# Attention's orders on ScalarE and SyncE, and pooling's first inputs loaded during attention

## The chip, the cores and the metric

The kernel runs on 1 core of a Trainium2 chip. The metric is the device time of one execution, in microseconds (us), with all inputs in HBM and the output written back to HBM. Runs differ by a few tenths of a per cent, so a median of several stands for a kernel.

## What is computed

One layer of a hybrid encoder on 2048 tokens of width 1024, in float32: three token mixers side by side (pooling, differential attention, a state-space layer), gates from the same normalised input, an output projection, and then a mixture of experts.

```python
h = modulate(rmsnorm(x, norm1_g[l]), sh1, sc1)
u_a, q, k, v, u_c = jnp.split(h @ w_in[l], splits, axis=-1)
ya = pool_mixer(u_a, pool_w[l], pool_scale[l])
yb = diff_attention(q, k, v, cos, sin, ...)          # 4 heads, 2 maps each, block-causal
yc = ssm_mixer(u_c, ...)
ga, gb, gc = jnp.split(jax.nn.sigmoid(h @ gate_w[l] + gate_b[l]), 3, axis=-1)
mixed = ga * (ya @ proj_a[l]) + gb * (yb @ proj_b[l]) + gc * (yc @ proj_c[l])
x = x + g1[:, None, :] * (mixed @ w_out[l])
x = x + g2[:, None, :] * hier_moe(h2, ...)           # top-1 group, top-2 experts
```

Attention, for a query block of 128 tokens: both maps are a softmax over the keys that the mask allows, a = p0 - lam * p1, and the result is a @ v. Pooling, for a group of 64 channels with window w of 2, 4, 8 or 16: the mean of the last w tokens minus the token, times a 64x64 matrix, times a scale per channel:

```python
cnt = jnp.minimum(t, float(w))[None, :, None]
outs.append((cg - prev) / cnt - ug[:, :, g])
y = jnp.einsum('bsgc,gcd->bsgd', pooled, pool_w).reshape(B, S, POOL_WIDTH)
return y * pool_scale
```

## The kernel before

The program is a chain of stages: projection, attention, pooling, state space, merge and output, experts. Each stage has one instruction stream per engine, written out by hand, with semaphores between the engines, and it ends with a barrier of all engines. An engine works strictly in the order of its stream, so an instruction that waits holds up all that stand behind it.

**Attention** runs over 4 heads (h = 0 to 3) and in each over 16 blocks of 128 queries (i = 0 to 15, called blocks 0 to 15 here). A block's keys come in chunks of 512. For a block TensorE makes the scores of both maps (L303), VectorE evacuates them and takes the maxima (L518, L521, `maxima` L529 and L530), ScalarE takes the exponentials of map 1 and map 0 (`exps`, L427), VectorE weighs the maps against each other (`weigh`, L542), TensorE turns the result by 128x128 blocks (`turn_a`, L313), ScalarE copies a chunk of turned blocks (`place`, L435), and TensorE multiplies them by v (`weigh_v`, L324). `take` (L440, L443) reads the block's result, and at a head's end all 16 are normed (L486), turned, split into a high and a low part and stored by SyncE as y. The scores of block i + 2 and the exponentials of block i + 1 stand inside block i.

**Gates fill TensorE's gaps.** The gate matmul goes by columns of 128 outputs (24 columns, c) and halves of 512 tokens: a gate unit (48 in attention, `gu`) is 8 groups of 3 matmuls (L336 to L338, high by high, high by low, low by high) that sum in one PSUM bank, bank 7. `gate_plan` gives in `slots[i]` how many groups stand in block i: the first number ahead of the block's turns, and then one for each chunk of keys, behind the turn of that chunk. A unit can't begin before ScalarE has read bank 7 (`gate_out`, L418). After each second unit `gate_out` also rounds the next column's weights to their high part (`w_high`, L412); VectorE then makes the low part (`lower`, L555), and SyncE may load the raw column after that (`load_w`, L248, 512 KB into one buffer). SyncE stores each gate output (`store_gates`, L256).

In block 3 the last group of unit 3 stands behind the only turn, and in block 14 the last group of unit 8 stood in the second chunk's slot (behind the second chunk's `turn_a` and ahead of the first chunk's `weigh_v`). In block 15 the last group of unit 9 stands in the third chunk's slot.

**SyncE** issues all the loads and stores, in one queue. Per head it goes over 12 gate units (u = 0 to 11). At u = 8 it waits for all scores of the head and loads q and k of the next one (16 loads, 4 MB; in the last head the late half of h, 4 MB). At u = 11 it stores y. At the stage's end it clears 128 rows of `acc` in HBM (512 KB) and waits for everything that is under way.

**Pooling** has two blocks of 128 channels (c = 0, 1), each of 2048 tokens. VectorE makes the window sums by doubling (`wider`, L814, L815) and the difference (L830 to L835). TensorE multiplies each 512 tokens by a 128x128 matrix with two 64x64 blocks in it (L788), ScalarE scales (L804) and rounds (L806), VectorE makes the low part (L840), SyncE stores both. Six gate units fill TensorE here too (`GateFill`): units 0 and 1 ahead of block 0's products, units 2, 3 and 4 ahead of block 1's, unit 5 at the end. Unit 2 is the first to use the late half of h. `GateFill.out` reads a unit out and, after each second one, calls `higher` for the next raw column (`gw_hi`); GpSimd makes the low part (`lower`, L691), and only then does SyncE load another (`load_next`, L652). SyncE's stream began with: u block 0 (1 MB), late half of h (2 MB high, 2 MB low), the scales (256 values), four 64x64 matrices, u block 1 (1 MB), a raw gate column, two blocks of uc (1 MB each).

## Time and profile before

| what | us |
|---|---|
| median of 3 runs (lowest, highest) | 2951.82 (2948.14, 2960.63) |
| the profiled execution, its own time | 2954.11 |
| its span (first to last instruction) | 2952.2 |
| TensorE busy in the span | 2782.0 (94%) |
| VectorE, ScalarE, GpSimd busy | 1905.2, 1469.0, 369.0 |
| granted TensorE clock, mean | 0.968 of full speed |

By stage, TensorE was busy for 607.37 of 631 us in attention (469 to 1100), not at all between 1100 and 1106 (the change of stages), for 45.65 of 57 us in pooling (1107 to 1164), and for 1695.84 of the 1788 us behind. Over attention the clock was at 0.99 of full speed, over pooling at 0.88.

A row of the views in order of time has the start in us from the span's start, the length in us, the engine, the line, the operation, output <- input, and the count; in brackets stands how long the engine had been idle before it, and whose instruction ended that. PE is TensorE's matmuls, PEld its weight loads, DVE VectorE, ACT ScalarE, POOL GpSimd, SPq SyncE's queue of transfers. Matmuls are pipelined, so a matmul of 512 columns shows 0.39 us but starts 0.23 us after the one before.

### The profile page before, as it was taken

To read this page: it belongs to the slowest core of one execution; us is meant where nothing else is said; L and a number is where in the kernel's file an instruction comes from. 1 tells how busy PE (TensorE), PEld (TensorE's weight loads), DVE (VectorE), ACT (ScalarE), POOL (GpSimd) and SP (SyncE) were. 2 spreads that over 40 slices of the span, in tenths; PEclk is the share of its full clock that TensorE was granted. 3 is DMA by queue.
4 is the path that set the end of the run, shared out by engine and by line. 5 is a ranking of instruction groups with operands and counts; after the bars stand their busy time and mean duration, and the time that the engine had idled before them with its cause. 6 is when DMAs were issued, how large, how long until landed. Compare 5 with 4: busy or idle time off the path is not lost. (4 is left out here: it accounts for less than half of the span.)

```text
span 2952.2 us, 41275 instructions
## 1 busy us (share of the span) xinstructions
PE 2782.0 (94%) x13642; PEld 2215.4 (75%) x13643; DVE 1905.2 (65%) x3149; ACT 1469.0 (50%) x2361; POOL 369.0 (13%) x287
## 2 busy tenths in 40 slices
PE   6999998999999988999998999987999999999996
PEld 5768886787877776788876878875777777777774
DVE  6754774746464655644455773457888888888884
ACT  4414664656565553233244342124666666666662
POOL 2101220000000001101010001110222222222211
PEclk8999999999999998999999999998999999999998
DMA  6475324040403137211148995428989989777884
GB/s 234 143 248 193 105 103 164 23 155 31 154 30 129 44 125 237 68 47 50 51 168 295 352 343 204 168 93 301 337 280 298 374 299 304 239 226 228 283 258 134
DMA packets 287584, 554.82 MB, mean 188 GB/s; under 512 B 28748, under 2 KB 95564, under 8 KB 285144
## 3 DMA queue, kind: packets, MB, share of 16 engines
q1 hardware_dynamic: 269048, 492.06, 46.7%
q0 software_dynamic: 14400, 52.44, 7.2%
q10 hardware_dynamic: 4000, 8.53, 0.9%
q8 instruction: 82, 1.34, 0.2%
q14 instruction: 54, 0.44, 0.1%
HBM read 418.21 MB, written 143.15 MB: 190 GB/s over the span
## 5 line engine op out<-in xcount | busy, mean ns | idle before, releaser
L2715 DVE TENSOR_TENSOR moe_w_lo<-moe_W,moe_w_hi 128x1024 fp32r<-128x1024 f32 x384 | 460.4, 1219 | 85.6 <-ACT moe_w_hi L2643 71.7
L2643 ACT CAST moe_w_hi<-moe_W 128x1024 fp32r (+1 forms) x384 | 402.0, 1052 | 148.1 <-PE moe_h1b L2566 76.2
L1631 PE MATMUL project_bank<-h_lo,w_hi 128*128 128x512 f32 x512 | 201.0, 393 | 0.0
L336 PE MATMUL att_bank<-h_hi,w_hi 128*128 128x512 f32 x384 | 168.9, 440 | 13.0 <-ACT att_gates L418 8.1
L2591 PE MATMUL moe_yb<-moe_W,moe_hT 128*128 x384 | 172.5, 592 | 0.0
L427 ACT ACTIVATE att_S<-att_S,att_nm,q_scale 128x128 f32<-128x128 f32 (+15 forms) x128 | 165.7, 1296 | 4.4 <-DVE att_nm L530 4.0
L2564 PE MATMUL moe_h1b<-moe_w_hi,moe_xT_hi 128*128 128x512 f32 x384 | 155.9, 406 | 4.8 <-DVE moe_xT_lo L2726 4.8
L521 DVE TENSOR_SCALAR_CACHE_REDUCE att_S<-att_bank 128x512 f32<-128x512 f32 x192 | 122.3, 687 | 54.8 <-PE att_bank L303 54.8
L338 PE MATMUL att_bank<-h_hi,w_lo 128*128 128x512 f32 x384 | 151.4, 394 | 0.0
L337 PE MATMUL att_bank<-h_lo,w_hi 128*128 128x512 f32 x384 | 151.2, 394 | 0.0
L2566 PE MATMUL moe_h1b<-moe_w_hi,moe_xT_lo 128*128 128x512 f32 x384 | 151.1, 393 | 0.0
L2565 PE MATMUL moe_h1b<-moe_w_lo,moe_xT_hi 128*128 128x512 f32 x384 | 151.0, 393 | 0.0
L2566 PE MATMUL moe_h3b<-moe_w_hi,moe_xT_lo 128*128 128x512 f32 x384 | 149.6, 389 | 0.0
L2564 PE MATMUL moe_h3b<-moe_w_hi,moe_xT_hi 128*128 128x512 f32 x384 | 149.4, 389 | 0.0
L2565 PE MATMUL moe_h3b<-moe_w_lo,moe_xT_hi 128*128 128x512 f32 x384 | 149.4, 389 | 0.0
L324 PEld LDWEIGHTS att_bank<-att_val,att_aT 128*128 128x128 f32 x1088 | 137.7, 191 | 14.1 <-ACT att_aT L435 5.1
L324 PE MATMUL att_bank<-att_val,att_aT 128*128 128x128 f32 x1088 | 145.0, 278 | 1.2 <-ACT att_aT L435 1.2
L698 ACT ACTIVATE gate_out<-ssm_gate_bank,gate_bias 128x512 f32<-128x512 f32 x42 | 28.9, 687 | 211.8 <-PE ssm_gate_bank L714 209.6
L2720 DVE TENSOR_TENSOR moe_w_lo<-moe_W,moe_w_hi 128x1024 fp32r<-128x1024 f32 x96 | 117.2, 1222 | 25.6 <-ACT moe_w_hi L2650 24.7
L435 ACT COPY att_aT<-att_bank 128x512 f32<-128x512 f32 (+3 forms) x160 | 82.8, 517 | 99.8 <-PE att_bank L313 99.3
L2591 PEld LDWEIGHTS moe_yb<-moe_W,moe_hT 128*128 128x128 f32 x384 | 72.6, 189 | 72.8 <-issue 69.0
L303 PE MATMUL att_bank<-shared 64*128 64x512 f32 (+2 forms) x960 | 124.3, 388 | 2.3 <-DVE att_S L521 2.3
(498 smaller groups left out, 6866.8 us busy)
## 6 DMA issues: line engine op xcount, KB each, us to landing
moe_W<-in_moe_w SPq DMA_DIRECT2D x96, 2048.0 KB, 13.8
w_raw<-in_gate_w SPq DMA_DIRECT2D x48, 512.0 KB, 3.8
out_sg<-gateT SPq DMA_DIRECT2D x32, 768.0 KB, 6.9
gateT<-att_gates SPq DMA_DIRECT2D x48, 256.0 KB, 2.0
gateT<-gate_out SPq DMA_DIRECT2D x48, 256.0 KB, 2.0
early<-in_ada_w SPq DMA_DIRECT2D x8, 1024.0 KB, 12.7
project_spare<-in_x SPq DMA_DIRECT2D x16, 512.0 KB, 6.9
zT<-project_oz SPq DMA_DIRECT2D x32, 256.0 KB, 3.5
```

Source lines behind the costliest of these rows:

```text
L324: mm = pe.matmul(bank[6][:, 0:P], aT[:, n % 2, j, :], val[:, 4 * c + j, :], start=4 * c + j == 0, stop=4 * c + j == i)
L336: pe.matmul(bank[7][:], w_hi[b][:, k, :], h_hi[:, k, at], start=k == 0, stop=False)
L337: pe.matmul(bank[7][:], w_hi[b][:, k, :], h_lo[:, k, at], start=False, stop=False)
L338: mm = pe.matmul(bank[7][:], w_lo[b][:, k, :], h_hi[:, k, at], start=False, stop=k == KD - 1)
L427: nc.scalar.activation(S[:, at, m, :n], S[:, at, m, :n], ACT.Exp, bias=nm[:, at, m:m + 1], scale=g["q_scale"][:, item // NT, item % NT, m: ...
L1631: pe.matmul(bank[n % 4][:], w_hi[b][:, k, :], low[:, k, at512(tb)], start=False, stop=False)
L2564: pe.matmul(to[:], xT_hi[:, k, :], w_hi[:, at, part], start=k == 0, stop=False)
L2565: pe.matmul(to[:], xT_hi[:, k, :], w_lo[:, at, part], start=False, stop=False)
L2566: mm = pe.matmul(to[:], xT_lo[:, k, :], w_hi[:, at, part], start=False, stop=k == KD - 1)
L2591: mm = pe.matmul(yb[nh][:], hT[:, k - KS, :], raw_2(at_raw, k, nh * 512, 512), start=False, stop=k == KF - 1)
L2643: nc.scalar.copy(w_hi[:, slot(p, first), :], raw(at, p)).then_inc(q["w13_high"], 1)
L2715: nc.vector.tensor_tensor(w_lo[:, own, :], raw(at, p), w_hi[:, own, :].bitcast(F32), ALU.subtract).then_inc(q["w1_low" if p < 4 else "w3_l ...
```

## The change

- ScalarE: in blocks 0 to 3 of each head both exponentials of the next block stand right behind `place`, ahead of the gate output. `w_high` is taken out of `gate_out` into `next_high`, with the same place everywhere but block 15, where it stands behind the next `place`.
- TensorE: one gate group of block 14 moves from the second chunk's slot to the first's, so ScalarE's gate output moves too. (In `slots[14]` the second and third numbers change places.)
- SyncE in attention: the load of the next raw column stands at the start of a unit (`next_w`), so at u = 8 it comes ahead of the q and k loads. At u = 5 of head 1 SyncE loads pooling's matrices and scales. At u = 1 of head 3, where there is no v left to load, it loads pooling's u block 0, into the place of vT, and clears the rows of `acc`.
- Pooling: u block 0, matrices and scales are there; SyncE's stream begins with u block 1, the late half of h, the raw column, uc. On ScalarE `higher` for the second raw column stands behind block 0's copies instead of ahead of them.
- Places in SBUF: vT, the matrices and the scales lie in tiles that both stages hold, and `first` and two empty rooms are sized so that the rest lies where it did.

```diff
@@ gate_plan
-             [1, 0, 1, 1, 0], [1, 0, 1, 1, 0], [1, 0, 1, 2, 1], [2, 1, 1, 1, 0]]
+             [1, 0, 1, 1, 0], [1, 0, 1, 1, 0], [1, 1, 0, 2, 1], [2, 1, 1, 1, 0]]
@@ attention, tiles
-        vT = s.sb("vT", [P, T])
+        s.sb("vT_room", [P, T])
+        vT = pool_in["u0"]
@@ attention, SyncE
+                def next_w(gu):
+                    if gu % 2 == 0:
+                        sp.wait_ge(q["w_split"], gu // 2 + 1)
+                        load_w(gu // 2 + 2)
+
                 def store_gates(gu):
                     c = gu // 2
-                    if gu % 2 == 0:
-                        sp.wait_ge(q["w_split"], c + 1)
-                        load_w(c + 2)
                     sp.wait_ge(q["gate_placed"], gu + 1)
...
                 for h in range(HEADS):
                     for u in range(NU):
+                        next_w(NU * h + u)
                         if u == units_by(NT - 3):
...
                         store_gates(NU * h + u)
-                        if u == 1 and h + 1 < HEADS:
+                        if h == 1 and u == 5:
+                            sp.wait_ge(q["pool_zeroed"], 1)
+                            for gr in range(4):
+                                at = slice((gr % 2) * 64, (gr % 2) * 64 + 64)
+                                sp.dma_start(pool_in["w"][at, gr // 2, at], g["pool_w"][0, gr]).then_inc(q["pool_ready"], 16)
+                            cols(nc, sp, pool_in["scale"][:], g["pool_scale"], 2, q["pool_ready"])
+                        if u == 1:
                             sp.wait_ge(q["v_turned"], TB * (h + 1))
-                            load_v(h + 1)
+                            if h + 1 < HEADS:
+                                load_v(h + 1)
+                            else:
+                                sp.dma_start(vT[:], g["zT"][0]).then_inc(q["u0_ready"], 16)
+                                sp.dma_start(g["acc"][T:T + P, :]..., zero[:]...).then_inc(q["cleared"], 16)
                 sp.wait_ge(q["raw_ready"], 16 * HEADS * CH)
-                sp.dma_start(g["acc"][T:T + P, :]..., zero[:]...).then_inc(q["cleared"], 16)
                 sp.wait_ge(q["cleared"], 16)
+                sp.wait_ge(q["u0_ready"], 16)
+                sp.wait_ge(q["pool_ready"], 16 * 5)
@@ attention, ScalarE
                         for n in range(lo, hi):
                             place(h, n)
+                            if high_after:
+                                next_high(high_after)
+                                high_after = 0
+                            if i < 4:
+                                exps(item + 1, 1)
+                                exps(item + 1, 0)
                             done += slots[i][1 + n - lo]
                             while placed < done // KD:
                                 gate_out(placed)
+                                if i == NT - 1:
+                                    high_after = placed
+                                else:
+                                    next_high(placed)
                                 placed += 1
-                            if n == lo and i + 1 < NT:
+                            if n == lo and 4 <= i < NT - 1:
                                 exps(item + 1, 1)
-                            if n == min(lo + 1, hi - 1) and i + 1 < NT:
+                            if n == min(lo + 1, hi - 1) and 4 <= i < NT - 1:
                                 exps(item + 1, 0)
@@ pooling, SyncE
-                sp.dma_start(ua[:, 0, :], g["zT"][0]).then_inc(u_ready[0], 16)
+                sp.dma_start(ua[1][:], g["zT"][1]).then_inc(u1_ready, 16)
                 sp.dma_start(h_hi[1][:].bitcast(F32), ...).then_inc(h_ready, 16)
                 sp.dma_start(h_lo[1][:].bitcast(F32), ...).then_inc(h_ready, 16)
-                cols(nc, sp, ps_col[:], g["pool_scale"], 2, small)
-                sp.wait_ge(zeroed, 1)
-                for gr in range(4):
-                    at = slice((gr % 2) * 64, (gr % 2) * 64 + 64)
-                    sp.dma_start(pw[at, gr // 2, at], g["pool_w"][0, gr]).then_inc(small, 16)
-                sp.dma_start(ua[:, 1, :], g["zT"][1]).then_inc(u_ready[1], 16)
                 fill.load_next(sp, 0)
@@ pooling, TensorE and ScalarE
-                    if n == 0:
-                        pe.wait_ge(small, 16 * 5)
...
                     if tb == 0:
+                        if c == 1:
+                            fill.higher(act, 1)
                         for u in ((0, 1), (2, 3, 4))[c]:
-                            fill.out(act, u)
-                    if n == 0:
-                        act.wait_ge(small, 16 * 5)
+                            fill.out(act, u, split=u != 1)
```

What stands in a row, at three places. First ScalarE in block 3 of head 1 (`att_S` of 128x640 are block 4's exponentials, `att_aT` is the copy of the turned blocks). Before:

```order
L443 ACTIVATE att_osq,att_ss<-att_bank,att_rec 128x128
L435 COPY att_aT<-att_bank 128x512
L418 ACTIVATE att_gates<-att_bank,gate_bias 128x512
L412 CAST w_hi<-w_raw 128x1024
L427 ACTIVATE att_S,att_den<-att_S,att_nm,q_scale 128x640 x2
L440 ACTIVATE att_o<-att_bank,att_rec 128x128
L443 ACTIVATE att_osq,att_ss<-att_bank,att_rec 128x128
```

and with the change:

```order
L464 ACTIVATE att_osq,att_ss<-att_bank,att_rec 128x128
L456 COPY att_aT<-att_bank 128x512
L448 ACTIVATE att_S,att_den<-att_S,att_nm,q_scale 128x640 x2
L437 ACTIVATE att_gates<-att_bank,gate_bias 128x512
L431 CAST w_hi<-w_raw 128x1024
L461 ACTIVATE att_o<-att_bank,att_rec 128x128
L464 ACTIVATE att_osq,att_ss<-att_bank,att_rec 128x128
```

The two exponentials of 128x640 moved ahead of the gate output and the cast.

Second TensorE in block 14 of head 0 (`h_hi`, `h_lo`, `w_hi`, `w_lo` are a gate group, `consts,att_S` a turn with one matmul for each 128x128, `att_val,att_aT` the product with v). Before:

```order
L337 MATMUL att_bank<-h_lo,w_hi 128x512
L338 MATMUL att_bank<-h_hi,w_lo 128x512
L313 MATMUL att_bank<-consts,att_S 128x128 x8
L336 MATMUL att_bank<-h_hi,w_hi 128x512
L337 MATMUL att_bank<-h_lo,w_hi 128x512
L338 MATMUL att_bank<-h_hi,w_lo 128x512
L324 MATMUL att_bank<-att_val,att_aT 128x128 x4
L313 MATMUL att_bank<-consts,att_S 128x128 x4
L336 MATMUL att_bank<-h_hi,w_hi 128x512
L337 MATMUL att_bank<-h_lo,w_hi 128x512
```

and with the change:

```order
L356 MATMUL att_bank<-h_lo,w_hi 128x512
L357 MATMUL att_bank<-h_hi,w_lo 128x512
L332 MATMUL att_bank<-consts,att_S 128x128 x4
L355 MATMUL att_bank<-h_hi,w_hi 128x512
L356 MATMUL att_bank<-h_lo,w_hi 128x512
L357 MATMUL att_bank<-h_hi,w_lo 128x512
L332 MATMUL att_bank<-consts,att_S 128x128 x4
L343 MATMUL att_bank<-att_val,att_aT 128x128 x4
L332 MATMUL att_bank<-consts,att_S 128x128 x4
L355 MATMUL att_bank<-h_hi,w_hi 128x512
```

The gate group moved from behind the two turns to between them.

Third ScalarE at pooling's start. Before:

```order
L698 ACTIVATE gate_out<-pooling_gate_bank,gate_bias 128x512 x2
L684 CAST gw_hi<-w_raw 128x1024
L804 ACTIVATE pooling_ya<-pooling_bank,pooling_ps_col 128x512
L806 CAST pooling_ya_hi<-pooling_ya 128x512
L804 ACTIVATE pooling_ya<-pooling_bank,pooling_ps_col 128x512
L806 CAST pooling_ya_hi<-pooling_ya 128x512
L804 ACTIVATE pooling_ya<-pooling_bank,pooling_ps_col 128x512
```

and with the change:

```order
L733 ACTIVATE gate_out<-pooling_gate_bank,gate_bias 128x512 x2
L829 ACTIVATE pooling_ya<-pooling_bank,pool_scale_in 128x512
L831 CAST pooling_ya_hi<-pooling_ya 128x512
L829 ACTIVATE pooling_ya<-pooling_bank,pool_scale_in 128x512
L831 CAST pooling_ya_hi<-pooling_ya 128x512
L829 ACTIVATE pooling_ya<-pooling_bank,pool_scale_in 128x512
L831 CAST pooling_ya_hi<-pooling_ya 128x512
L829 ACTIVATE pooling_ya<-pooling_bank,pool_scale_in 128x512
L831 CAST pooling_ya_hi<-pooling_ya 128x512
L719 CAST gw_hi<-w_raw 128x1024
L733 ACTIVATE gate_out<-pooling_gate_bank,gate_bias 128x512 x2
```

The cast `gw_hi` moved from ahead of block 0's four pairs of scale and cast to behind them.

## Rows read from the trace of the kernel before

**Rows 1.** Who waited, TensorE, attention and pooling: us in total, times, longest.
```profile
PE att_bank L313 <- DVE att_S L542: 9.6, 4, 2.4
PE att_bank L336 <- ACT att_gates L418: 8.1, 7, 1.4
...
PE pooling_bank L788 <- DMA pooling_pw<-in_pool_w: 6.0, 1, 6.0
```

**Rows 2.** In order of time, ScalarE, head 1, block 3: start, us, instruction.
```profile
658.11 0.59 ACT L435 COPY att_aT<-att_bank 128x512 f32<-128x512 f32 x1 [1.12 <-PE att_bank L313]
662.35 0.69 ACT L418 ACTIVATE att_gates<-att_bank,gate_bias 128x512 f32<-128x512 f32 x1 [3.65 <-PE att_bank L338]
662.94 1.04 ACT L412 CAST w_hi<-w_raw 128x1024 fp32r<-128x1024 f32 x1
...
664.79 0.91 ACT L427 ACTIVATE att_S<-att_S,att_nm,q_scale 128x640 f32<-128x640 f32 x1
```

**Rows 3.** In order of time, TensorE, head 1, turn of block 4.
```profile
667.22 0.66 PE L313 MATMUL att_bank<-consts,att_S 128*128 128x128 f32 x4 [2.41 <-DVE att_S L542]
```

**Rows 4.** In order of time, VectorE, head 1, around the weighing of block 4.
```profile
661.01 0.08 DVE L518 DVE_READ_ACCUMULATOR2_ANT att_mx<- 128x1 f32 x1
...
666.28 0.89 DVE L542 SCALAR_TENSOR_TENSOR att_S<-att_S,att_rec 128x640 f32<-128x640 f32 x1
```

**Rows 5.** In order of time, TensorE and its weight loads, head 1, blocks 14, 15.
```profile
757.87 0.50 PE L336 MATMUL att_bank<-h_hi,w_hi 128*128 128x512 f32 x1 [1.40 <-ACT att_gates L418]
...
761.29 1.72 PE L324 MATMUL att_bank<-att_val,att_aT 128*128 128x128 f32 x14
...
770.90 0.97 PEld L324 LDWEIGHTS att_bank<-att_val,att_aT 128*128 128x128 f32 x8 [0.17 <-ACT att_aT L435]
```

**Rows 6.** In order of time, ScalarE, head 1, block 14.
```profile
754.58 2.10 ACT L427 ACTIVATE att_S<-att_S,att_nm,q_scale 128x2048 f32<-128x2048 f32 x1
...
759.79 0.58 ACT L435 COPY att_aT<-att_bank 128x512 f32<-128x512 f32 x1
```

**Rows 7.** Who waited, SyncE's queue, attention and pooling.
```profile
SPq L256 <- ACT att_gates L418: 364.2, 44, 20.9
...
SPq L286 <- DMA gateT<-att_gates: 2.3, 1, 2.3
...
SPq L235 <- DMA acc<-att_zero: 1.5, 1, 1.5
```

**Rows 8.** In order of time, SyncE's queue, pooling's start.
```profile
1108.31 6.75 SPq L615 DMA_DIRECT2D pooling_ps_col<-in_pool_scale  x1
```

**Rows 9.** In order of time, TensorE, pooling.
```profile
1106.86 0.77 PE L712 MATMUL pooling_gate_bank<-shared,w_hi 128*128 128x512 f32 x1 [7.15 <-PEq L141]
...
1119.23 0.39 PE L714 MATMUL pooling_gate_bank<-shared,w_lo 128*128 128x512 f32 x1
...
1133.84 0.96 PE L712 MATMUL pooling_gate_bank<-late_hi,w_hi 128*128 128x512 f32 x1
...
1150.77 4.22 PE L788 MATMUL pooling_bank<-pooling_ua,pooling_pw 128*128 128x512 f32 x8
```

**Rows 10.** In order of time, ScalarE, pooling.
```profile
1129.30 1.04 ACT L684 CAST gw_hi<-w_raw 128x1024 fp32r<-128x1024 f32 x1 [8.96 <-DMA w_raw<-in_gate_w]
```

**Rows 11.** In order of time, VectorE, pooling.
```profile
1112.53 0.15 DVE L814 COPY pooling_A<-pooling_ua 128x1 f32<-128x1 f32 x1 [15.97 <-DMA pooling_ua<-zT]
...
1123.55 0.17 DVE L835 COPY pooling_first<-pooling_ua 128x16 f32<-128x16 f32 x1
1127.60 0.15 DVE L814 COPY pooling_A<-pooling_ua 128x1 f32<-128x1 f32 x1 [3.87 <-DMA pooling_ua<-zT]
...
1132.64 2.21 DVE L814 COPY pooling_A<-pooling_B 128x4 f32<-128x4 f32 x1
...
1145.71 0.17 DVE L835 COPY pooling_first<-pooling_ua 128x16 f32<-128x16 f32 x1
```

**Rows 12.** Transfers, pooling: issuer, count, KB each, us from issue to landing.
```profile
late_lo<-late_lo SPq DMA_DIRECT2D x1, 2048.0 KB, 17.0
```

More of the change, by code:

```diff
@@ L229, in stage_attention @@
                  "v_turned v_placed scored evacuated maxed exped scaled weighed a_turned a_placed "
-                 "summed o_copied o_squared o_rooted o_normed o_turned o_placed o_split y_stored lam_ready lam cleared late").split()
+                 "summed o_copied o_squared o_rooted o_normed o_turned o_placed o_split y_stored lam_ready lam cleared late pool_zeroed pool_ready u0_ready").split()
         q = {n: s.sem(n) for n in names}
@@ L287, in _ @@
                 sp.wait_ge(q["y_stored"], 32 * HEADS)
+            @block.gpsimd
+            def _(pool):
+                nc.gpsimd.memset(pool_in["w"][:], 0.0).then_inc(q["pool_zeroed"], 1)
             @block.tensor
@@ L692, in lower, with out @@
                                      self.tiles["w_hi"][b][:].rearrange("p k n -> p (k n)").bitcast(F32), ALU.subtract).then_inc(self.w_split, 1)
-    def out(self, act, u):
+    def out(self, act, u, split=True):
         act.wait_ge(self.summed, u + 1)
@@ L699, in out @@
                                   bias=self.tiles["gb"][:, self.c0 + self.unit(u)[0]:self.c0 + self.unit(u)[0] + 1]).then_inc(self.placed, 1)
-        if u % 2 == 1 and u // 2 + 1 < self.count:
+        if split and u % 2 == 1 and u // 2 + 1 < self.count:
             self.higher(act, u // 2 + 1)
@@ L787, in _ @@
                         pe.wait_ge(placed, n - 1)
-                    pe.matmul(bank[n % 2][:], pw[:, c, :], ua[:, c, tb * 512:(tb + 1) * 512], start=True, stop=True).then_inc(mixed, 1)
+                    pe.matmul(bank[n % 2][:], pw[:, c, :], ua[c][:, tb * 512:(tb + 1) * 512], start=True, stop=True).then_inc(mixed, 1)
                 for k in range(KD):
@@ L816, in _ @@
                 for c in range(2):
-                    dve.wait_ge(u_ready[c], 16)
-                    u = ua[:, c, :]
+                    if c == 1:
+                        dve.wait_ge(u1_ready, 16)
+                    u = ua[c][:]
                     wider(A[:], u, 1)
@@ L2982, in program @@
                 pass
+            with nc.sbuf_tensor("pool_u0", [P, T], F32) as u0:
+                pass
             with nc.sbuf_tensor("h_lo1", [P, KD, T // 2], F32R) as h_lo1:
```

43 lines of the change are left out of this document (25 added, 18 removed).

## The prediction

> **What bounds the kernel now.** I read three views in this order: who waited for whom on TensorE (attention and pooling alone), then the instructions in order of time on TensorE, ScalarE and VectorE around each long wait, then SyncE's queue and the transfers. TensorE holds this kernel: in attention its instructions stand back to back, and only a handful of waits cut them, so a microsecond taken from such a wait is a microsecond of the program, as long as the next engine in line isn't late too. [rows 1] gives the waits that the change aims at: 9.6 us in four waits for VectorE's weighing, 8.1 us in seven for ScalarE's gate outputs, and 6.0 us in one for pooling's matrices. The kernel is a chain of stages, with a barrier between attention, pooling and the state-space stage. What pooling's end gains moves the rest forward whole, since everything behind starts from that barrier.
>
> **Part 1, the exponentials ahead of the gate in block 3 of each head.** In [rows 2] ScalarE has copied block 3's turned weights at 658.11 and then stands until TensorE ends a gate unit; gate output (0.69), cast (1.04) and two exponentials (0.91 each) follow, so the sums that VectorE waits for come at about 665.8. In [rows 4] VectorE weighs at 666.28 for 0.89, and in [rows 3] TensorE goes on at 667.22, after 2.41 idle. The maxima for these exponentials were ready long before. Placed right behind the copy (0.59 long) they run from 658.7 to about 660.9. VectorE has the scores of the block after to evacuate until 661.1 [rows 4], then weighs until about 662.5. TensorE arrives at 667.22 - 2.41 = 664.8, so the wait goes whole. The gate output isn't delayed: the exponentials end 1.4 us ahead of its 662.35. What is late next? TensorE's scores and ScalarE's next copy follow TensorE's own time and shift with it. Four heads: 4 x 2.41 = **9.6 us**. Bounds: 9.6, and 4 x 1.5 = 6 if VectorE or ScalarE, shifted against each other, give back a microsecond in each head.
>
> **Part 2, block 14: one gate group from slot 2 to slot 1, its output ahead of the exponential.** TensorE loses 1.40 to the gate output in each head [rows 5]. ScalarE's row [rows 6] shows why: a 2.10 exponential stands at 754.58, then a copy, then the gate output. In the new order TensorE turns four blocks (through at about 754.0, when ScalarE's copy ahead of 754.58 began), runs the gate group (0.7, an eighth of a unit of 5.6), and ScalarE, free at 754.6, waits for it until about 755.1, puts the gate out (0.69) and starts the exponential at about 755.7. That is 1.1 later than 754.58. One gate output no longer stands between the two exponentials (0.6), so the rest of the queue is 0.55 later: the third copy begins not at 759.79 [rows 6] but at about 760.35, and ends at 760.95. TensorE needs it for the 14 products that start at 761.29 [rows 5]; 1.40 earlier would be 759.9. So it waits there instead, and starts at about 761.05. I keep 0.25 a head, **1.0 us** in all, with bounds of 0 and 4 x 1.4 = 5.6 us. Block 15's weights are ready at about 763.3, TensorE turns them at about 764.0: no wait there.
>
> **Part 3, block 15: the cast behind the copy.** TensorE's weight load waited 0.17 for that copy [rows 5]; 4 x 0.17 = **0.7 us**, between 0 and 0.7.
>
> **Part 4, SyncE's queue in attention.** The raw columns are loaded before the score wait and the 4 MB of q and k instead of behind them: nobody waits for them now, so nothing is gained or lost. The matrices and scales enter in head 1: the scales' issue alone holds the queue for 6.75 us [rows 8], the four matrix loads come on top. Behind them are the next raw column and the next gate stores. SyncE's cover is its waits for ScalarE's gate outputs, 364.2 us in 44, the longest 20.9 [rows 7]; without it the cost would be some 10 us once. The block of u (1 MB) and the cleared rows (512 KB) go out early in head 3, where the gate stores are the only traffic: nothing. The new tile places alone cost nothing: same sizes, same engines.
>
> **Part 5, the end of attention.** SyncE waited 2.3 us for the last gate store and then 1.5 us more for the cleared rows [rows 7]. The second goes: **1.5 us**, bounds 1.0 and 2.0.
>
> **Part 6, pooling.** I count from TensorE's first instruction, t = 0 at 1106.86 [rows 9]. Now: gate units 0 and 1 end at t = 12.7, TensorE waits 6.04 for the matrices [rows 1], then ScalarE stands 8.96 us until 1129.30 on a raw column queued behind everything else [rows 10], while four pooled products need its copies, and unit 2 starts at 1133.84, t = 27.0 [rows 9]. After the change:
> - VectorE starts at t = 0.2; now it waits to 1112.53 for u. Its chain for block 0 takes 1112.53 to 1123.72, 11.2 us [rows 11], so t = 11.4. GpSimd's lowering now runs beside it, at t = 1 to 5. In the other chain a 128x4 copy beside GpSimd took 2.21 us, where one of 128x16 takes 0.17 [rows 11]; I add 2.0, t = 13.4. The Trainium skill (GPSIMD Engine Reference, the quick-facts table) says that GpSimd's SBUF interfaces are shared with VectorE; by it the 2.0 stay, without it the products start at t = 12.7, and the sum is the same, because the next item ends last.
> - The second pooling block (eight matmul rows with their copies) takes 4.2 us [rows 9]. So the first is through at about t = 17.6.
> - Unit 2 needs the late half of h, two loads of 2 MB. The second took 17.0 us to land [rows 12]; it was issued just ahead of the scales' load at 1108.31 [rows 8], so it landed at t = 17.0 to 18.4, and I take 17.9. The 1 MB in front stays (it is now the other block of u). What changes is what is queued behind it: the raw column and uc now follow at t = 5 rather than 12. Bounds: 17 if the queue serves in order, and 22 if all 7.5 MB queued by then share the time. I take the first kind, since u, issued 0.5 us ahead of the 4 MB, was there at t = 5.7 [rows 11]. The Trainium skill (DMA: Bandwidth & Descriptors, Queues, rings and completion order) says each engine takes its descriptors in ring order; by it the 22 is excluded, and the sum is as forecast.
> - So unit 2 starts at t = 18.0 instead of 27.0: **9.0 us**, bounds 5.0 and 10.0.
> - Behind it: ScalarE's cast of the raw column follows the four copies at about t = 20, GpSimd has lowered it by about 25; unit 4 needs it at t = 29. VectorE's second chain takes 1127.60 to 1145.88, 18.3 us [rows 11], so it ends at t = 31.7, and TensorE wants it after three units (1133.84 to 1150.77, 16.9 us [rows 9]), at t = 34.9. The margin is 3.2 us, against 4.9 now.
>
> **The sum.** 9.6 + 1.0 + 0.7 + 1.5 + 9.0 = 21.8 us. The profiled execution took 2954.1 (span 2952.2), so 2932.3; against the median of 2951.8 it is 2930.0. I say **2931**. All of it lies in attention and pooling; the stages behind should show nothing.
>
> **The rivals.**
> A. The late half of h binds, and later than I say. For it: transfers are the densest thing in pooling, and more is queued at once. Against it: u's early landing. With h at t = 22, pooling gives 5.0 and the total 17.8; with 6 from part 1 as well, 14 us, 2940.
> B. The order of block 14 pays in full, since ScalarE gains time elsewhere (parts 2 and 5 at their upper ends, pooling at t = 17): 4.6 + 0.5 + 1.0 more, 28 us, 2926 from the profiled time and 2924 from the median.
> C. Slower: SyncE is stuck in head 1. The scales are 256 separate 4-byte elements. If SyncE's queue doesn't get past them before ScalarE needs raw column 11, ScalarE's cast waits, and TensorE behind it. The cover in one place is up to 20.9 us [rows 7]; each microsecond beyond it is one of the program. From 43 us on (20.9 + 21.8) the whole gain is gone, and an issue of 90 us would give 2954 + 47, about 3001. [rows 8] shows 6.75.
> D. The change doesn't do what it says: the exponentials in block 3 still come late, because what they wait for is not ScalarE's order but their maxima. Then 9.6 goes and 12.2 are left: 2940 to 2942. Against it: VectorE's evacuation at 661.01 is of the block after.
>
> **Chances.** Forecast (2924 to 2937) 0.72, A 0.12, B 0.06, D 0.07, C 0.03. A measurement of this kernel can tell about 0.5%, 14.8 us, from no change. A, D and the weak edge of the forecast lie near that bound: faster 0.83, within it 0.14, slower 0.03. The range runs from 2920 (B, from the fastest run shown, 2948) to 2944 (A and D, from a slower start): those leave out C and the combination of A with D.
>
> **What would show it.** On TensorE: no wait of 2.4 us ahead of the turn of block 4 in any head, and in block 14 a wait for the copy of about 1 us where the one for the gate output was. Last attention matmul some 11 us earlier. From it to pooling's first matmul about 5.6 us instead of 7.15. In pooling VectorE starts with the stage, no wait for matrices, and unit 2 at t = 18, released by the load of h. Part 6 is wrong if unit 2 starts after t = 20, or if TensorE waits for VectorE's second chain; part 2 if the new wait is missing (then up to 4.6 us more) or if a wait of over 1.4 us appears. The forecast as a whole is wrong if a stage behind pooling changes its length by more than 3 us.

## The result, and the profile after

The changed kernel takes 2925.9 us (median of 5 runs, 2924.8 to 2933.9) against 2951.8 (2948.1 to 2960.6). The ratio is 0.9912, with a 95% interval of 0.9898 to 0.9927: 26 us, 0.9% faster. The forecast was 2931 with a range of 2920 to 2944, so time and sign were right. Part of that is luck, since two misses of the sum cancel each other in part. By stages it was right less evenly, as this table of the two profiled executions shows. "Attention" runs from its first matmul to the end of its last, "pooling" from its first matmul to the state-space stage's first.

| stretch | before | after | change | forecast |
|---|---|---|---|---|
| to attention's first matmul | 468.8 | 464.3 | -4.5 | 0 |
| attention | 631.0 | 612.7 | -18.3 | -11.3 |
| attention's last to pooling's first matmul | 7.15 | 5.89 | -1.3 | -1.5 |
| pooling | 57.3 | 51.1 | -6.2 | -9.0 |
| everything behind | 1788.1 | 1789.1 | +1.0 | 0 |
| span | 2952.2 | 2923.0 | -29.2 | -21.8 |

TensorE's waits in attention and pooling, with the change (us in total, times, longest), are the answer to [rows 1]:

```profile
PE ssm_bank L999 <- PEq L141: 7.2, 1, 7.2
PE pooling_gate_bank L747 <- PEq L141: 5.9, 1, 5.9
...
PE att_bank L343 <- ACT att_aT L456: 3.3, 12, 0.4
PE att_bank L355 <- ACT att_gates L437: 2.6, 3, 0.9
PE att_bank L322 <- DVE att_S L556: 2.3, 4, 0.6
```

The line of 9.6 us for VectorE's weighing is gone, and so are pooling's matrices. Of the 8.1 us for gate outputs 2.6 are left (three heads' first unit). New are 3.3 us for ScalarE's copies (1.2 before), and the wait of 7.2 us ahead of the state-space stage, which had been 3.7.

ScalarE in order of time in block 3 of head 1, the answer to [rows 2]:

```profile
648.54 0.59 ACT L456 COPY att_aT<-att_bank 128x512 f32<-128x512 f32 x1 [1.12 <-PE att_bank L332]
649.02 0.92 ACT L448 ACTIVATE att_S<-att_S,att_nm,q_scale 128x640 f32<-128x640 f32 x1
...
649.94 0.91 ACT L448 ACTIVATE att_S<-att_S,att_nm,q_scale 128x640 f32<-128x640 f32 x1
...
652.78 0.69 ACT L437 ACTIVATE att_gates<-att_bank,gate_bias 128x512 f32<-128x512 f32 x1 [1.84 <-PE att_bank L357]
```

The two exponentials (L448) follow the copy at once and end at 650.85; the gate output comes 1.9 us later, when TensorE has ended its unit, and was not delayed. VectorE in the same place, the answer to [rows 4]:

```profile
651.88 0.88 DVE L577 SCALAR_TENSOR_TENSOR att_S<-att_S,att_rec 128x640 f32<-128x640 f32 x1
```

It is through at 652.8, before TensorE turns the block at 655.08, without a wait.

### The profile page after: what moved, and what is told of

The parts are those of the page before. It is cut to its first block and busy times, and to the rows that moved or that the text cites. A ratio compares the mean times of both kernels' runs of the same rounds, so it can differ in the third digit from the quotient of the medians.

```text
span 2923.0 us, 41275 instructions
## 1 busy us (share of the span) xinstructions
PE 2774.7 (95%) x13642; PEld 2209.9 (76%) x13643; DVE 1907.6 (65%) x3149; ACT 1468.3 (50%) x2361; POOL 372.4 (13%) x287
## 5 line engine op out<-in xcount | busy, mean ns | idle before, releaser
L448 ACT ACTIVATE att_S<-att_S,att_nm,q_scale 128x128 f32<-128x128 f32 (+15 forms) x128 | 165.8, 1296 | 4.5 <-DVE att_nm L565 4.0
L726 POOL TENSOR_TENSOR w_lo<-w_raw,w_hi 128x1024 fp32r<-128x1024 f32 x15 | 38.5, 2568 | 876.0 <-ACT w_hi L719 876.0
```

What stands on the lines that cost most here:

```text
L448: nc.scalar.activation(S[:, at, m, :n], S[:, at, m, :n], ACT.Exp, bias=nm[:, at, m:m + 1], scale=g["q_scale"][:, item // NT, item % NT, m: ...
```

## The experiments

Stage lengths in us, from the profile of each kernel, and the medians. All but the first two are the changed kernel with the edits told below. "Start of attention" is the time to its first matmul, "to pooling" that from its last matmul to pooling's first. The medians come from several chips, so kernels are compared by their ratios, each to the kernel before on its own chip, wherever the chips differ.

| kernel | start of attention | attention | to pooling | pooling | median (runs) | ratio to before, 95% |
|---|---|---|---|---|---|---|
| before, first profile | 468.8 | 631.0 | 7.15 | 57.3 | 2951.8 (5) | |
| before once more | 468.3 | 630.2 | 7.15 | 58.0 | 2953.0 (10) | 0.9988 to 1.0018 |
| changed | 464.3 | 612.7 | 5.89 | 51.1 | 2925.9 (5) | 0.9898 to 0.9927 |
| exponentials back | 464.6 | 628.5 | 5.86 | 51.1 | 2941.4 (8) | 0.9941 to 0.9971 |
| block 14 back | 465.6 | 615.0 | 5.86 | 51.0 | 2926.4 (4) | 0.9878 to 0.9924 |
| all attention orders back | 468.2 | 633.5 | 5.85 | 51.1 | 2946.1 (10) | 0.9957 to 0.9984 |
| exponentials back, waits filled | 467.6 | 622.9 | 5.85 | 51.0 | 2935.9 (4) | 0.9918 to 0.9959 |
| pooling's cast ahead | 468.0 | 613.3 | 5.88 | 53.5 | 2928.9 (4) | 0.9902 to 0.9938 |
| low parts early | 461.7 | 612.8 | 5.88 | 49.7 | 2919.3 (4) | 0.9874 to 0.9916 |
| low parts early, unit 5 split | 469.0 | 614.8 | 5.87 | 48.1 | 2923.7 (4) | 0.9877 to 0.9922 |
| raw column behind | 465.1 | 613.3 | 5.87 | 50.9 | 2927.2 (4) | 0.9897 to 0.9947 |
| clearing at the end | 468.3 | 612.2 | 7.51 | 51.0 | 2930.9 (4) | 0.9909 to 0.9960 |
| u block 0 in pooling | 468.7 | 615.7 | 5.89 | 53.6 | 2929.6 (4) | 0.9911 to 0.9952 |

**What moves without an edit.** The kernel before, run again:

> The kernel before once more, for what moves without an edit. The changed kernel's profile reached its first attention matmul 4.5 us earlier (464.28 against 468.75), in a stage with no edit. Theory: that is the spread between executions, so this profile's start lies anywhere in 463 to 470, while the attention stage itself (first to last matmul) is 631 us again, within 2. Rival: the new places of tiles in SBUF speed up the projection; then this profile starts attention at 468 to 469 again.

Attention began at 468.3, which by this one profile would have spoken for the rival. But over all the kernels here, of which none but the first two differs from the changed one ahead of attention, it begins anywhere between 461.7 and 469.0. Most of that spread is the granted clock: by the clock records of the traces TensorE lost between 9.6 and 15.4 us to half clock ahead of attention (15.4 in the kernel before, 10.4 in the changed one), and the start less this loss is 452 to 455 us in all thirteen profiles. So the 4.5 us ahead of attention are taken for the spread of single executions, and not for a gain of the change; the medians agree, since the three edited stretches alone give 18.3 + 1.3 + 6.2 = 25.8 us of the 25.9. With two profiles of the old tile places a mean difference of a microsecond or two isn't excluded. Everything behind pooling, edited nowhere either, took 1783.3 to 1793.8 us. So a stage in the middle is compared with itself, not by its place in the span.

**Exponentials back.**

```diff
                             place(h, n)
...
-                            if i < 4:
-                                exps(item + 1, 1)
-                                exps(item + 1, 0)
...
-                            if n == lo and 4 <= i < NT - 1:
+                            if n == lo and i + 1 < NT:
                                 exps(item + 1, 1)
-                            if n == min(lo + 1, hi - 1) and 4 <= i < NT - 1:
+                            if n == min(lo + 1, hi - 1) and i + 1 < NT:
                                 exps(item + 1, 0)
```

> The changed kernel with block 0 to 3's exponentials back behind the gate output. Theory: the four waits of 2.4 us return, and in the heads in which the granted clock falls to 1.2 GHz after the wait another 1.5 to 2 us, so attention is 9.6 + 3 to 6 = 13 to 16 us longer than with the change, 2939 to 2942. Rival (the prediction's sum): the waits alone, 9.6 us, clock at full behind them, 2935.5.

Attention takes 15.8 us more (628.5 against 612.7), the medians differ by 15.5. The waits are the old ones (total, times, longest):

```profile
PE att_bank L332 <- DVE att_S L574: 9.6, 4, 2.4
```

So 6.2 us come on top of the 9.6. The busy time by stretch tells from where: behind the stretch's length stand the busy us (and the number of instructions) of TensorE, its weight loads, VectorE, ScalarE and GpSimd, then the granted clock, the share of the DMA engines and GB/s. Behind the wait of head 2:

```profile
817.98:819.98 2.00, 2.00 (x14) 1.68 (x16) 1.56 (x4) 1.31 (x2) 0.00 (x0) 0.84 0.00 0
819.98:821.98 2.00, 2.00 (x8) 1.27 (x7) 2.00 (x8) 0.29 (x2) 0.00 (x0) 0.50 0.69 201
821.98:823.98 2.00, 2.00 (x10) 1.60 (x9) 0.01 (x1) 0.67 (x2) 0.00 (x0) 0.81 0.24 69
```

TensorE is busy all the time there, at 0.84, 0.50 and 0.81 of full speed. The same in the kernel before, head 2, whose first stretch is the wait itself:

```profile
820.77:823.17 2.40, 0.00 (x0) 0.00 (x0) 1.32 (x4) 1.58 (x6) 0.00 (x0) 1.00 0.00 0
823.17:825.17 2.00, 2.00 (x10) 1.50 (x12) 1.31 (x3) 1.17 (x2) 0.00 (x0) 0.60 0.00 0
825.17:827.17 2.00, 2.00 (x10) 1.38 (x9) 1.50 (x5) 0.43 (x2) 0.00 (x0) 0.55 0.71 207
827.17:829.17 2.00, 2.00 (x12) 1.60 (x11) 0.77 (x4) 0.70 (x2) 0.00 (x0) 1.00 0.23 64
```

In four microseconds at 0.60 and 0.55 of full speed 1.7 us of matmuls are lost. By the clock records it is one stretch of 3.4 us at half speed. The waits of 2.41 us are the same in all four heads of all four kernels that have them; the clock fell to the 1.2 GHz level behind three in the kernel before, two in its second profile, three here and all four with all orders back: 12 of 16. Three falls lose 3 x 1.7 = 5.1 us, which leaves 1.1 of the 6.2; a first wait for v at attention's start that was 0.6 longer in this profile is part of it.

**The waits filled.** Whether the idle time does it, or something else at that place, is told apart by taking the idle time away without the wait: TensorE turns a constant 16 times while it would wait.

```diff
+                        if i == 4:
+                            pe.wait_ge(q["a_placed"], NP * h + lo - 1)
+                            for _ in range(16):
+                                pe.transpose(bank[4 + lo % 2][:, :P], const(g, "ident"), const(g, "ident"))
                         pe.wait_ge(q["weighed"], NT * h + i + 1)
```

> The kernel of e1_no_exps (exponentials of blocks 0 to 3 back behind the gate output) with 16 turns of a constant, whose result nobody reads, on TensorE ahead of each of the four long waits, into the bank that the next turn overwrites. Theory (the wait of 2.4 us costs itself, and then the granted clock): the waits shrink to about 0.4 us by idle time but TensorE goes on at the same moment as in e1_no_exps, and the granted clock stays at 1.0 behind all four. Attention then takes 612.7 + 9.6 = 622.3 us instead of 628.5, the kernel 2935. Rival: the clock falls for another reason (the mix of work behind, or by the hour), then attention takes 628 to 630 again.

Attention takes 622.9 us, 0.6 from the forecast. TensorE, head 2, the 16 extra turns and what follows:

```profile
815.89 1.91 PE L399 MATMUL att_bank<-consts 128*128 128x128 f32 x16
818.46 0.66 PE L332 MATMUL att_bank<-consts,att_S 128*128 128x128 f32 x4 [0.66 <-DVE att_S L578]
```

and the stretches around it:

```profile
816.00:818.00 2.00, 1.80 (x17) 1.56 (x15) 0.86 (x3) 1.64 (x7) 0.00 (x0) 1.00 0.03 8
818.00:820.00 2.00, 1.54 (x12) 1.25 (x14) 1.77 (x4) 0.84 (x2) 0.00 (x0) 1.00 0.00 0
820.00:822.00 2.00, 2.00 (x16) 1.46 (x12) 1.86 (x7) 0.76 (x2) 0.00 (x0) 1.00 0.41 115
```

The real work goes on no sooner, since VectorE is as late as it was, but the clock stays at 1.00, here and behind the other three waits. The useless work made attention 5.6 us shorter than without it, and the three falls that are gone account for 5.1 of that. So of the 15.8 us some 10 are the waits and some 5 the clock. The stage lengths and the clock show this; the ratios of the two kernels (0.9939 and 0.9956) point the same way, but their intervals overlap.

**Block 14 back.**

```diff
-             [1, 0, 1, 1, 0], [1, 0, 1, 1, 0], [1, 1, 0, 2, 1], [2, 1, 1, 1, 0]]
+             [1, 0, 1, 1, 0], [1, 0, 1, 1, 0], [1, 0, 1, 2, 1], [2, 1, 1, 1, 0]]
```

> The changed kernel with block 14's gate group back in its slot. By the changed kernel's rows (0.17 + 0.37 of new waits where 1.40 was) 4 x 0.86 = 3.4 us come back: 2929.3. By the prediction's sum it would be 1.0 us: 2926.9.

Attention takes 2.3 us more, and the four waits of 1.4 for the gate output are back (8.1 in seven), the eight new ones for copies gone (1.2 in four). The medians differ by 0.5, which settles nothing, and attention itself varies by 3.5 us among kernels with the same order (612.2 to 615.7). That variation has a place: the two longest (614.8 and 615.7) waited 1.6 and 2.2 us for v at attention's start, with a fall of the clock behind it, the others 1.2 or less, without one. So the size is read from the stretch that the edit touches, from block 14's first gate group to the next head's first scores. In head 1, with block 14 back:

```profile
742.40 0.48 PE L355 MATMUL att_bank<-h_hi,w_hi 128*128 128x512 f32 x1
...
761.56 0.95 PE L322 MATMUL att_bank<-shared 64*128 64x128 f32 x12
```

and with the change:

```profile
740.47 0.48 PE L355 MATMUL att_bank<-h_hi,w_hi 128*128 128x512 f32 x1
...
759.04 0.95 PE L322 MATMUL att_bank<-shared 64*128 64x128 f32 x12
```

That is 19.16 and 18.57 us, and the other heads differ by 0.55 to 0.57 in the same stretch: 2.3 us in all. The idle time changed by 0.85 a head, close to the theory's 0.86, but this overstates the gain, since around the two new waits TensorE loses more than shows as idle (the 14 products behind the second take 1.83 us, where [rows 5] has 1.72). Neither the 3.4 nor the prediction's 1.0 came true. In the kernel before, and with all orders back, head 1's stretch takes 19.36 and 19.32, so the cast of block 15 is worth 0.2 a head.

ScalarE with the change, head 1, block 14:

```profile
742.59 0.69 ACT L437 ACTIVATE att_gates<-att_bank,gate_bias 128x512 f32<-128x512 f32 x1
...
747.81 0.96 ACT L456 COPY att_aT<-att_bank 128x512 f32<-128x512 f32 x2
```

and TensorE:

```profile
745.88 1.16 PE L343 MATMUL att_bank<-att_val,att_aT 128*128 128x128 f32 x8 [0.17 <-ACT att_aT L456]
...
748.44 1.83 PE L343 MATMUL att_bank<-att_val,att_aT 128*128 128x128 f32 x14 [0.37 <-ACT att_aT L456]
```

The gate output starts at 742.59, 0.1 us behind the copy and not 0.5: TensorE's group had begun at 741.61, before ScalarE started its copy (741.89). So the third copy (747.81) is 5.2 us behind the gate output's start, and TensorE waits for it 0.37, and 0.17 for the second.

**All attention orders back** (the exponentials' and block 14's edits above, and the cast of block 15 back in `gate_out`'s place):

```diff
-                                if i == NT - 1:
-                                    high_after = placed
-                                else:
-                                    next_high(placed)
+                                next_high(placed)
```

> The changed kernel with all of ScalarE's and TensorE's attention orders undone (exponentials, block 14, cast of block 15); SyncE's queue, the early loads and pooling stay changed. Theory: attention as long as before but for the last wait, 18 us more than the change, 2944; the parts add up (exponentials 13 to 16, block 14 3.4, cast 0.7). Rival: SyncE's new order carries a share, then this comes out at 2940 or less although the single undoings sum to 18.

Attention takes 20.8 us more than with the change. That is 2.5 more than in the kernel before, with the same waits and all four falls of the clock, the last of them longer than any other (0.50 for more than six microseconds). The single undoings add to 18.1, with the cast's 0.8 to 18.9. The four falls lose 8.5 us here, against 5.1 with the exponentials alone back, which more than covers the rest. The rival is out: the kernel takes 2946.1, not 2940 or less. What is left of the change, the early loads, the clearing and pooling, is worth 6.5 us by the medians (2946.1 against 2952.5 for the kernel before on the same chip), and by the ratio's interval 5 to 13.

**Raw column behind.** SyncE's new order alone undone:

```diff
                 def store_gates(gu):
                     c = gu // 2
+                    next_w(gu)
                     sp.wait_ge(q["gate_placed"], gu + 1)
...
-                        next_w(NU * h + u)
```

> The changed kernel with the load of the raw gate column back behind SyncE's waits and its 4 MB of q and k. The prediction costed this edit at nothing: attention stays at 612.7 us within 1.5. Rival: the raw column's late landing (15 us in the kernel before) made ScalarE's cast late somewhere, then attention is 1 to 3 us longer.

Attention takes 613.3 us: the edit costs nothing, as forecast.

**Clearing at the end.** The store of the cleared rows stands behind the last gate store again.

> The changed kernel with the cleared rows of acc stored at attention's end again. By the prediction 1.5 us between the stages come back: 5.9 to 7.1 or 7.4 us from attention's last matmul to pooling's first. Rival: the last gate store lands at the same time anyway, the gap stays within 0.3 of 5.9.

It takes 7.51 us from stage to stage, 1.6 more, and 0.1 above the theory. SyncE's queue waits there (total, times, longest) as in [rows 7]:

```profile
SPq L301 <- DMA gateT<-att_gates: 2.1, 1, 2.1
SPq L236 <- DMA acc<-att_zero: 1.6, 1, 1.6
```

**Pooling's cast ahead.**

```diff
-                        if c == 1:
-                            fill.higher(act, 1)
                         for u in ((0, 1), (2, 3, 4))[c]:
-                            fill.out(act, u, split=u != 1)
+                            fill.out(act, u)
```

> The changed kernel with ScalarE's cast of pooling's second raw column back ahead of block 0's copies. The raw column was issued at 1087.57 and finished issuing at 1090.8, behind 5 MB; if it lands at t = 19 (1102), the cast stands there, block 0's four products wait for their copies, unit 2 starts at t = 23 to 24 instead of 17.4. But since the stage's end hangs on the stores of y by the changed kernel's rows (7.2 us from TensorE's last matmul to the next stage, 3.7 before), up to 3.5 us of it are hidden. Theory: the stage takes 51.1 + 2.5 to 3.5 us. Rival: the stage's end moves by the whole 6 us.

ScalarE's cast, the answer to [rows 10], waited 5.07 us rather than 8.96, since the column was asked for earlier:

```profile
1105.66 1.04 ACT L719 CAST gw_hi<-w_raw 128x1024 fp32r<-128x1024 f32 x1 [5.07 <-DMA w_raw<-in_gate_w]
```

TensorE's work in the stage grew by 6.0 us, and its gap behind shrank from 7.2 to 3.7, so the stage is 2.4 longer, just under the theory's 2.5 to 3.5 and far from the rival's 6. The order of the cast is worth 6 us to TensorE and 2.4 to the program.

**u block 0 in pooling.** The load of zT[0] goes from head 3 of attention to the head of SyncE's stream in pooling, with a wait of VectorE for it; matrices and scales stay early.

```diff
+                sp.dma_start(ua[0][:], g["zT"][0]).then_inc(u0_ready, 16)
                 sp.dma_start(ua[1][:], g["zT"][1]).then_inc(u1_ready, 16)
```

> The changed kernel with pooling's u block 0 loaded at pooling's start (1 MB ahead of u block 1), matrices and scales still early. Theory: VectorE starts at t = 5.7 instead of 0, everything that hangs on its two chains comes 4 to 6 us later: block 0's products wait for it at t = 13.7 to about 18, and the stage takes 55 to 57 us instead of 51.1. Rival: the matrices and scales were what pooling gained from (TensorE waited for them by name in the kernel before), then the stage stays under 53.

The stage takes 53.64 us against 51.06, 2.6 more: less than the theory's 4 to 6 and not the rival's "under 53" either. VectorE's start and TensorE's block 0:

```profile
1095.63 0.15 DVE L839 COPY pooling_A<-pool_u 128x1 f32<-128x1 f32 x1 [14.41 <-DMA pool_u<-zT]
```
```profile
1106.89 5.48 PE L813 MATMUL pooling_bank<-pool_u,pool_w_in 128*128 128x512 f32 x8 [3.93 <-DVE pooling_first L860]
```

VectorE starts 5.4 us later, but then no lowering of GpSimd falls into its first chain, which takes 11.2 us and not 13.2. TensorE waits 3.9 for it, and the gap behind gives 1.6 back. I had the direction, and not these two refunds.

**Low parts early.** The test of what now sets pooling's end. VectorE makes block 0's four low parts inside its chain for block 1:

```diff
                         wider(A[:], B[:], 4)
+                        for n in range(4):
+                            low(n)
...
-                for n in range(8):
+                for n in range(4, 8):
+                    low(n)
```

(`low(n)` is the old loop's body, the wait for `y_high` and the subtraction.)

> The changed kernel with VectorE's four low parts of pooling's block 0 inside its chain for block 1 (behind the third doubling) instead of behind the chain. Theory (the stage's end hangs on 16 stores of y that begin only at 1117): the first eight stores go out at 1112, the end of TensorE's work to the next stage falls from 7.2 to about 3.7 us; the chain ends 2.5 us later, TensorE waits some 2 us for it. Stage 51.1 to 49.6, kernel 1.5 faster, 2924. Rival (TensorE's work sets the end, the gap is only a late barrier): the gap stays at 7 and the stage is 2 us longer.

TensorE's waits, and the first store of y in SyncE's queue:

```profile
PE ssm_bank L1003 <- PEq L141: 3.7, 1, 3.7
...
PE pooling_bank L813 <- DVE pooling_first L868: 2.6, 2, 2.2
```
```profile
1110.04 0.43 SPq L788 DMA_DIRECT2D y_hi<-pooling_ya_hi  x1
```

The first store goes out at t = 29.7, counted from pooling's first matmul, where the changed kernel's goes at t = 34.3. The gap is 3.7 again, TensorE waits 2.2 us for the longer chain, the stage takes 49.7. As forecast.

**Low parts early, unit 5 split:** the same, and four of unit 5's eight groups ahead of block 1's products.

```diff
+                    if n == TB:
+                        for k in range(4):
+                            fill.group(pe, 5 * KD + k)
                     pe.wait_ge(pooled, c + 1)
...
-                for k in range(KD):
+                for k in range(4, KD):
                     fill.group(pe, 5 * KD + k)
```

> As e2_lo_early, and half of pooling's gate unit 5 (4 of 8 groups) ahead of block 1's products, where TensorE waited for VectorE. Theory: TensorE has no wait, its last matmul is at t = 43.9 as in the changed kernel, and the gap behind it is 3.7 to 5: stage 47.6 to 49, kernel 2 to 3.5 us faster than the change. Rival: GpSimd's lowering and VectorE slow each other more, TensorE waits for the chain all the same, no gain over e2_lo_early.

```profile
PE ssm_bank L1006 <- PEq L141: 4.6, 1, 4.6
...
PE pooling_bank L816 <- DVE pooling_first L871: 0.3, 1, 0.3
```

TensorE's wait for VectorE is 0.3, the gap 4.6, the stage 48.1: 2.9 shorter than with the change, as the theory had it. Both kernels are faster than the kernel before (ratios of 0.9895 and 0.9900). Against the changed kernel's 0.9912 their intervals overlap, so what they gain over it is shown by the length of the stage alone. By the medians the first is the faster of them (2919.3 against 2923.7), by the stage's length the second. Single executions differ by up to 7 us ahead of attention, where neither has an edit, and only 4.3 lie between the medians of four runs, so their order stays open.

## Why the prediction was right, and where it wasn't

**Part 1, right on the mechanism, too small.** The forecast was 9.6 us, and all four waits went, with nothing late behind them. The sum counted a wait as what it shows, 2.41. It costs 2.41 and, three times in four here, 1.7 more, since TensorE works for 3.4 us at half its clock. The rows were there to be read. Block 4's scores behind the wait, in heads 0 and 1 of the kernel before:

```profile
510.78 2.46 PE L303 MATMUL att_bank<-shared 64*128 64x512 f32 x12
...
667.81 1.50 PE L303 MATMUL att_bank<-shared 64*128 64x512 f32 x12
```

I read [rows 3], the one head of the kernel before in which the clock did not fall, and multiplied by four. Attention gave 18.3 us: 9.6 by part 1's waits, 5.1 by the clock's three falls, 2.3 by part 2 and 0.8 by part 3, with 0.5 left open. Of the 7.0 beyond the forecast the clock is 5.1 and part 2 is 1.3. The filled kernel shows the clock's part on its own.

**Part 2, right mechanism, wrong size.** A new wait for the copy took part of the gain, as said, but 0.37 us, with 0.17 for the second copy, instead of 1.15. The order gave 2.3 us and not 1.0. The step that failed is the 0.5 us that ScalarE was to stand between its copy and the gate output: it stood 0.1.

**Part 3** gave 0.8, forecast 0.7: with block 14 back the stretch read above takes 0.2 us less in each head than with all orders back, and in that stretch the two differ by the cast alone. **Part 4** cost nothing. Rival C was far off, and more so than [rows 8] said:

```profile
677.97 2.40 SPq L286 DMA_DIRECT2D pool_w_in<-in_pool_w  x4
680.41 0.59 SPq L650 DMA_DIRECT2D pool_scale_in<-in_pool_scale  x1
```

These are SyncE's queue in head 1, the matrices and the scales: the scales' issue took 0.59 us, against the 6.75 in [rows 8], where 5 MB of transfers were ahead of it. **Part 5** gave 1.3, forecast 1.5; putting the clearing back costs 1.6.

**Part 6, right up to unit 2, wrong behind.** TensorE with the change (t = 0 at 1082.85), the answer to [rows 9]:

```profile
1096.55 4.22 PE L813 MATMUL pooling_bank<-pool_u,pool_w_in 128*128 128x512 f32 x8
1100.21 0.79 PE L747 MATMUL pooling_gate_bank<-late_hi,w_hi 128*128 128x512 f32 x1
```

Block 0's products start at t = 13.7, unit 2 at t = 17.4; forecast 13.4 and 18.0. VectorE's chain ended at t = 13.2, as forecast, and held nobody up: TensorE came to the products without a wait, a microsecond later than in the kernel before, since in pooling's first 5.8 us the granted clock was 0.51 of full speed, against 0.71 there. The late half landed at t = 17.0 (1083.68 and 16.2), at the lower end of the bounds and 0.3 us before TensorE was free for it, so the sign "released by the load of h" didn't come true; block 0's products ended last. So TensorE's part of the stage is 9.8 us shorter, and the step that failed is "what pooling's end gains moves the rest forward whole", with unit 2 taken for the end. I followed TensorE to block 1's products and checked that VectorE's chain would come in time for them. It did, but by less than I said: it ended at t = 33.7 for a forecast of 31.7, and the products started at t = 34.1. What I didn't follow is what else stands behind that chain on VectorE: the low parts of block 0, and behind them on SyncE all 16 stores of y, 4 MB. VectorE, GpSimd, and SyncE's queue with the change:

```profile
1085.36 2.21 DVE L839 COPY pooling_B<-pooling_A 64x2 f32<-64x2 f32 x1
...
1103.77 4.47 DVE L840 TENSOR_TENSOR pooling_B<-pooling_A 64x2040 f32<-64x2040 f32 x1
...
1114.06 2.25 DVE L860 COPY pooling_u<-pooling_first 64x16 f32<-64x16 f32 x1
...
1116.43 2.49 DVE L866 TENSOR_TENSOR pooling_ya_lo<-pooling_ya,pooling_ya_hi 128x512 fp32r<-128x512 f32 x4
```
```profile
1083.94 3.60 POOL L726 TENSOR_TENSOR w_lo<-w_raw,w_hi 128x1024 fp32r<-128x1024 f32 x1 [619.39 <-ACT w_hi L719]
1103.70 2.40 POOL L726 TENSOR_TENSOR gw_lo<-w_raw,gw_hi 128x1024 fp32r<-128x1024 f32 x1 [16.15 <-ACT gw_hi L719]
1113.45 2.83 POOL L726 TENSOR_TENSOR w_lo<-w_raw,w_hi 128x1024 fp32r<-128x1024 f32 x1 [7.35 <-ACT w_hi L719]
```
```profile
1117.14 0.32 SPq L788 DMA_DIRECT2D y_hi<-pooling_ya_hi  x1
...
1128.41 0.63 SPq L789 DMA_DIRECT2D y_lo<-pooling_ya_lo  x1
1129.08 0.66 SPq L702 DMA_DIRECT2D gateT<-gate_out  x1
```

The first and the last store of y in SyncE's queue before:

```profile
1146.61 0.43 SPq L760 DMA_DIRECT2D y_hi<-pooling_ya_hi  x1
...
1158.17 0.64 SPq L761 DMA_DIRECT2D y_lo<-pooling_ya_lo  x1
```

Before, VectorE began the low parts 5 us ahead of block 1's products (1145.80 and 1150.77), the last stores of y followed the products' own copies, and the last gate store went out as soon as ScalarE had it ready (1161.21, issued at 1161.23). Now the first begins when block 1's products do (both at about 1117), they go out nearly back to back, at 0.3 to 1.0 us each, and the last gate store waits behind them until 1129.08, though ScalarE had it ready at 1127.4. The stage ends when they have landed. Two kernels show this: with the low parts early, and with pooling's cast ahead, the gap falls from 7.2 to 3.7. So 9.8 us of TensorE's time became 6.2 of the program's. The margin that I gave in the forecast, 3.2 us against 4.9, was the sign, read only for TensorE; what was left of it was 0.5.

The contention of VectorE and GpSimd stood in the forecast twice (2.0 us added to the first chain, and the 2.0 that the second chain's 18.3 us in [rows 11] already held) and came three times: VectorE's 64x2 copy took 2.21, its last doubling 4.47 and another copy 2.25, each beside a GpSimd lowering; their own lengths are 0.17, 2.28 and 0.17. The third is the some 2 us by which the second chain was late. The two copies ended when the lowering did (1087.57 and 1087.54, 1116.31 and 1116.28), and the doubling ended 2.1 us behind the lowering (1108.24 and 1106.10), about its own length. The Trainium skill (GPSIMD Engine Reference, Specifications) says that the two share SBUF interfaces, and the traces agree, with 2.0 to 2.2 us for each lowering of 1024 columns.

**The total.** The medians moved by 25.9 us, forecast 21.8. Part 1's missing clock (5.1 more) and part 2 (1.3 more) outweighed pooling's end (2.8 less). None of the rivals came true as such. The parts were off by more than the sum, and that the median came within 5 us of 2931 is luck in so far as these misses have opposite signs. The sign "a stage behind pooling changes its length by more than 3 us" could not have told anything: kernels with the same code there differ by 10 us.

## What to carry to other kernels

A wait on TensorE costs its length and, where the granted clock falls behind it, a second sum (here 1.7 us for 2.41 of idle time): read the clock of the stretches behind every wait of a repeated pattern, not of one, and where the wait can't go, filling it with useless matmuls can pay (here some 5 us in four waits). Price an order by the length of the stretch that it touches, not by the waits that go and come: here these said 3.4 us and the stretch 2.3. When an edit lets one engine reach a point earlier, follow every engine's stream from there to the barrier, the stores in the queue above all, since slack that was there for another engine is used up without a sign in that engine's waits. And compare a stage with itself: here 7 us of spread lay ahead of the first edited instruction and 10 us behind the last.

## What the runs showed of the hardware that I had not expected

- An idle time of 2.41 us in a stream that is otherwise full was enough in 12 of 16 cases for the granted clock to fall to half for 3.4 us (once 6.8); with the same wait filled but for 0.66 us it fell in none of four, and behind the 1.4 us idle in block 14 in none of 16.
- The issue of the same load of 256 single values took 6.75 us of SyncE's queue with some 5 MB under way and 0.59 in a quiet stretch, and it landed after 2.2 us instead of 15.4.
- A GpSimd subtraction of 128x1024 (2.4 us with VectorE idle) beside VectorE costs VectorE about 2.1 us once, on whatever instruction stands there, even one of 0.17.
